# A two-layer diffusion trunk on one Trainium2 core: the last down matrices loaded and used in halves, one token tile's expert rows summed by TensorE, the next norm inside the expert pass, and an opening loaded field by field

## The reference

```python
for i in range(DEPTH):                       # 2 layers
    sh1, sc1, g1, sh2, sc2, g2 = modulation(c, w_ada[i], b_ada[i])
    h = rmsnorm(x, norm_g[i, 0]) * (1 + sc1) + sh1
    y = hgrn2_mixer(h, ...) if i == 0 else diff_attention(...)
    x = x + g1 * y
    h = rmsnorm(x, norm_g[i, 1]) * (1 + sc2) + sh2
    x = x + g2 * hier_moe(h, ...)            # 16 experts, two for each token

def hier_moe(u, ...):                        # w_gate, w_up: (16, 1024, 512); w_down: (16, 512, 1024)
    h = silu(einsum('nd,edf->nef', xt, w_gate)) * einsum('nd,edf->nef', xt, w_up)
    h = h * combine[:, :, None]
    return einsum('nef,efd->nd', h, w_down)
```

## Time and profile before

| | us |
|---|---|
| median of 3 runs (lowest, highest) | 1240.55 (1237.82, 1240.55) |
| the profiled execution | 1240.84 |
| its span | 1239.0 |
| TensorE busy in the span | 1141.3 (92%) |
| VectorE busy | 428.6 (35%) |
| ScalarE busy | 225.6 (18%) |
| GpSimd busy | 136.1 (11%) |
| read from HBM | 304.67 MB |

### The profile page before, as it was taken

How to read it: one execution, slowest core, us unless ns; L and a number is a source line. 1 busy time by engine, 2 the same in 40 slices (tenths; PEclk the granted TensorE clock), 3 DMA queues, 4 the chain that set the end, 5 groups by cost and what they waited for, 6 DMA issues and landing times.

```text
span 1239.0 us, 20044 instructions
## 1 busy us (share of the span) xinstructions
PE 1141.3 (92%) x8612; PEld 681.9 (55%) x8612; DVE 428.6 (35%) x1108; ACT 225.6 (18%) x523; POOL 136.1 (11%) x219
## 2 busy tenths in 40 slices
PE   4999999998899999999989899998989899999885
PEld 2566666665444576666654444444545756666552
DVE  2155555555522350100003755307853420000007
ACT  2210101011111321011000311116632221011010
POOL 0343433333100000000002100000000000000012
PEclk9999999999899999999989899998999999999998
DMA  9973444434923348999999913226751279999993
GB/s 337 316 242 110 138 138 137 137 137 176 380 103 125 136 163 335 424 426 426 424 426 409 346 68 115 106 100 237 262 235 64 73 295 426 426 425 426 424 423 143
DMA packets 97601, 317.08 MB, mean 256 GB/s; under 512 B 3792, under 2 KB 38912, under 8 KB 81120
## 3 DMA queue, kind: packets, MB, share of 16 engines
q1 hardware_dynamic: 90160, 298.05, 62.8%
q10 hardware_dynamic: 5248, 10.97, 2.3%
q0 software_dynamic: 2096, 6.67, 1.5%
HBM read 304.67 MB, written 11.01 MB: 255 GB/s over the span
## 4 chain that ended last, share of the span: by engine, by line
issue 70%; PE 20%; DVE 3%; DMA 3%; POOL 1%; ACT 0%; POOLq 0%; DVEq 0%
PE bank L775 10%; PE bank L784 4%; DMA ring<-expert_rows,moe_row 2%; PE bank L800 2%; PE bank L470 1%; DVE ring L1666 1%; DMA ring<-in_w_ada 1%; PE bank L856 1%; PE bank L809 0%; DVE hg_kf L1759 0%; PE bank L849 0%; DVE uT L1664 0%; PE bank L867 0%; PE bank L476 0%; DVE uT L1676 0%
## 5 line engine op out<-in xcount | busy, mean ns | idle before, releaser
L665 PE MATMUL bank<-ring,xn 128*64 128x256 f32 x1536 | 175.4, 387 | 10.7 <-DMA ring<-in_moe_w_up 7.9
L665 PEld LDWEIGHTS bank<-ring,xn 128*64 128x64 f32 x1536 | 112.1, 140 | 76.5 <-issue 12.8
L775 PE MATMUL bank<-uT,ring 128*128 128x384 f32 x384 | 135.0, 496 | 0.9 <-DVE uT L1712 0.9
L971 PE MATMUL bank<-ring,uT 128*128 128x512 f32 x288 | 126.6, 595 | 1.3 <-issue 1.3
L1654 DVE TENSOR_TENSOR moe_hh<-xn,bank 128x256 f32<-128x256 f32 x32 | 13.5, 421 | 308.0 <-ACT xn L1151 307.9
L2019 POOL TENSOR_TENSOR moe_flag<-con 128x1 f32<-128x1 f32 x2 | 0.4, 192 | 850.8 <-DMA expert_rows<-xn 850.8
L654 PE MATMUL bank<-moe_g,moe_h 128*128 128x128 f32 x768 | 92.2, 277 | 0.4 <-DVE moe_g L1552 0.4
L775 PEld LDWEIGHTS bank<-uT,ring 128*128 128x128 f32 x384 | 69.2, 190 | 42.1 <-issue 2.0
L654 PEld LDWEIGHTS bank<-moe_g,moe_h 128*128 128x128 f32 x768 | 88.2, 192 | 6.1 <-issue 6.1
L971 PEld LDWEIGHTS bank<-ring,uT 128*128 128x128 f32 x288 | 53.9, 191 | 65.4 <-issue 65.4
L681 PE MATMUL bank<-ring,xn 128*64 128x512 f32 x384 | 85.0, 595 | 0.6 <-DMA ring<-in_moe_w_down 0.6
(11 more groups left out here) (269 smaller groups left out, 1306.2 us busy)
## 6 DMA issues: line engine op xcount, KB each, us to landing
ring<-in_w_ada SPq DMA_DIRECT2D x24, 2048.0 KB, 9.9
...
```

The source lines that it names most:

```text
L665: last = mm(bank[2 + e][64 * g:64 * g + 64, 256 * part:256 * part + 256], m["xe"][:, k, 64 * e:64 * e + 64], cols(slot)[:, k, 256 * g:256 ...
L775: last = mm(to[:, 0:TOK], w[:, k, f, :], uT[:, k, :], start=(k == 0), stop=(k == KC - 1))
L971: last = mm(bank[b % 2][:, :], uT[:, k, t * P:(t + 1) * P], cols(slot)[:, k, :], start=(k == 0), stop=(k == KC - 1))
```

## The change

- The eighth pair's two down matrices are loaded in four transfers instead of two: first the columns 0 to 511 of both, then the columns 512 to 1023 (`last_down`). A contiguous piece is 2 KB, where it was 8 KB. TensorE waits for the first two transfers (`down_half`), does the first half, then the last pair's products of the first half (`first_halves`), and waits for the other two before the second half. `keep_busy` ahead of it is 2 products instead of 6.
- The fetched rows of tile 1 are weighted and summed by TensorE: four products (`fetched_rows`) with diagonal matrices `rw` that VectorE builds beside the gate products. GpSimd adds nothing to x any more. VectorE does tile 0 first, then sums tile 2's rows, then finishes tiles 1 and 2 by halves.
- For the first layer the norm of the next layer stands in the pass: ScalarE squares each tile as it is done and takes the root, VectorE normalises, with the columns of the modulation made earlier. TensorE turns tile 0 behind the pass and tiles 1 and 2 within the first two products of the attention's input matrix; eight `keep_busy` products between are gone. ScalarE does both halves of tile 0's shift and scale.
- The first block of the attention's input matrix is issued when the gathers of tile 2 have landed, where it waited only for its buffer.
- The mean goes everywhere: the root takes the sum with a scale and a bias (`root_of`). In three places a root of a constant (`root_table`) stands ahead of the real one.
- Opening: head 0 is loaded as fields q and first gate, then modulation blocks 1 and 3, then the other two fields. TensorE takes block 1 before the head's products, and part 1's later blocks wait for pieces of `uT`.

The core of the diff:

```diff
+            def first_head(fields, landed):
+
+                src = a["hgrn_w_in"][0].rearrange("(k p) (f h n) -> p k f h n", p=P, f=5, h=HEADS)
+                for f in fields:
+                    sp.dma_start(head_cols(4)[:, :, f, :], src[:, :, f, 0, :]).then_inc(landed, 16)
...
+            def last_down(n, p):
+
+                for half in range(2):
+                    here = slice(512 * half, 512 * half + 512)
+                    for e in range(2):
+                        slot, use = expert_slot(n, PAIRS - 1, 4 + e)
+                        if half == 0:
+                            sp.wait_ge(*expert_free(n, PAIRS - 1, 4 + e, p))
+                        src = a["moe_w_down"][n, 2 * (PAIRS - 1) + e].rearrange("(k p) n -> p k n", p=P)
+                        sp.dma_start(down_rows(slot).rearrange("p g j n -> p (g j) n")[:, :, here], src[:, :, here])\
+                            .then_inc(S[n]["down_half"] if half == 0 else full[n][slot], 16)
+
             x_rows = x[:, :, :]
             sp.dma_start(x_rows[:, 0, :], a["x_prompt"][0]).then_inc(x_in, 16)
             sp.dma_start(x_rows[:, 1:3, :], a["x_sample"][0].rearrange("(t p) d -> p t d", p=P)).then_inc(x_in, 16)
             ada(0, 0, 0, 0)
             ada(0, 2, 2, 0)
-            head(0, 4, 0)
+            first_head((0, 2), first_in)
             ada(0, 1, 1, 0)
             ada(0, 3, 3, 0)
+            first_head((3, 1), full[0][4])
             sp.dma_start(masks[:, :, :].rearrange("p n t -> p (n t)"), a["const_mask"]).then_inc(heads_in, 16)
             sp.dma_start(HG["s0"][:, :, :], a["state_hgrn"][0, 0].rearrange("n h p v -> p (n h) v")).then_inc(heads_in, 16)
             head(1, 5, 0)
...
+                if b == 0:
+                    sp.wait_ge(S[0]["rows2"], count * 32)
+                elif slot == SLOT_ORDER[0][0]:
+                    sp.wait_ge(norm_act, count * (2 * T))
+                else:
+                    sp.wait_ge(used[0][slot], count * USES + uses_before[0][slot])
                 src = a["attn_w_qkv"][0].rearrange("(k p) (b n) -> p k b n", p=P, n=512)
                 sp.dma_start(cols(slot), src[:, :, b, :]).then_inc(full[1][slot], 16)
...
                     if i == PAIRS - 1:
-                        keep_busy(6, 512)
-                    rows_of = [down_rows(weights_in(i, 4 + e)) for e in range(2)]
+                        keep_busy(2, 512)
+                        pe.wait_ge(s["down_half"], at_pass[0] * 32 + 32)
+                        rows_of = [down_rows(expert_slot(n, i, 4 + e)[0]) for e in range(2)]
+                    else:
+                        rows_of = [down_rows(weights_in(i, 4 + e)) for e in range(2)]
                     for half in range(2):
+                        if half == 1 and i == PAIRS - 1:
+                            first_halves(it)
+                            for e in range(2):
+                                weights_in(i, 4 + e)
                         for g in range(2):
                             for j in range(2):
                                 for e in range(2):
...
+
+                def last_pair(t, half, start, stop):
+
+                    return mm(bank[LAST_BANKS[t][half]][:, :], m["wc"][:, t * P:(t + 1) * P], m["oe"][:, half, :],
+                              start=start, stop=stop)
+
+                def first_halves(it):
+
+                    pe.wait_ge(s["wc_ready"], at_pass[0] + 1)
+                    pe.wait_ge(s["oe_ready"], it * 2 + 1)
+                    last_pair(0, 0, True, True).then_inc(s["last_mm"], 1)
+                    last_pair(1, 0, True, False)
+                    last_pair(2, 0, True, True)
+
+                def fetched_rows(half):
+
+                    here = slice(512 * half, 512 * half + 512)
+                    for j, rows in enumerate((m["own"], second_rows[n])):
+                        done = mm(bank[LAST_BANKS[1][half]][:, :], m["rw"][:, j, :], rows[:, 1, here],
+                                  start=False, stop=(j == 1))
+                    return done
...
-                    pe.wait_ge(s["wc_ready"], p + 1)
                     pe.wait_ge(s["oe_ready"], p * (2 * PAIRS) + 2 * PAIRS)
-                    for t in range(T):
-                        for half in range(2):
-                            mine = mm(bank[LAST_BANKS[t][half]][:, :], m["wc"][:, t * P:(t + 1) * P], m["oe"][:, half, :],
-                                      start=True, stop=True)
-                        mine.then_inc(s["last_mm"], 1)
-
-                expert_passes(pe, n, before, body, after)
+                    last_pair(0, 1, True, True).then_inc(s["last_mm"], 1)
+                    last_pair(2, 1, True, True).then_inc(s["last_mm"], 1)
+                    last_pair(1, 1, True, False)
+                    pe.wait_ge(s["rows1"], p * 32 + 32)
+                    fetched_rows(0)
+                    fetched_rows(1).then_inc(s["last_mm"], 1)
+
+                return expert_passes(pe, n, before, body, after)
...
+            first_block(2, raw)
             proj(0, 0, 0, 0)
-            proj(0, 0, 0, 2)
-            first_block(2, raw)
             first_turn(2, raw)
             first_block(3, raw)
+            proj(0, 0, 0, 2)
             first_turn(3, raw)
             proj(0, 0, 0, 4)
-            need(pe, 0, "uT_act", T)
-            need(pe, 0, "uT_dve", T)
             for part in (1, 3, 5, 6, 7, 8):
                 proj(0, 0, 0, part)
...
             raw = AT["raw"]
-            keep_busy(8, 512)
-            for t, banks in enumerate(((6, 4), (2, 3), (5, 7))):
-                need(pe, 1, "xn_ready", t + 1)
-                turn_tile(1, "xT_done", xn, t, banks)
+            def turn_features(t):
+
+                pe.wait_ge(norm_dve, count * T + t)
+                turn_tile(1, "xT_done", xn, t, LAST_BANKS[t])
+
+            turn_features(0)
...
+            def root_of(to, sums, count):
+
+                return A(to, sums, ACT.Sqrt, bias=const("eps"), scale=1.0 / count)
+
...
+                def after(p):
+                    if n == 0:
+                        root_table()
+                        for t in range(T):
+                            act.wait_ge(s["added"], p * T + (T + t))
+                            A(second_rows[n][:, t, :], x[:, t, :], ACT.Square, accum_out=stat[:, 0, t:t + 1])\
+                                .then_inc(norm_act, 1)
+                            act.wait_ge(norm_act, p * (2 * T) + (2 * t + 1))
+                            root_of(stat[:, 2, t:t + 1], stat[:, 0, t:t + 1], D).then_inc(norm_act, 1)
+
+                return expert_passes(act, n, before, body, after)
...
+                        for j in range(2):
+                            v.tensor_scalar(m["rw"][:, j, :], ident, m["hw"][:, j, 1:2], None, ALU.mult)
...
+                    def gated_rows(t):
+
+                        other = second_rows[n][:, t, :]
+                        await_step(step(v.tensor_tensor(other, other, gates[:, SIDE[t], :], ALU.mult)))
+                        await_step(step(v.tensor_tensor(x[:, t, :], x[:, t, :], other, ALU.add)))
+
+                    def last_added(t, half):
+
+                        here = slice(512 * half, 512 * half + 512)
+                        other, last_pair = second_rows[n][:, t, here], bank[LAST_BANKS[t][half]][:, :]
+                        dve.wait_ge(s["last_mm"], p * LAST_MM + (2 + half, 5, 4)[t])
+                        if t == 2:
+                            await_step(step(v.tensor_tensor(other, other, last_pair, ALU.add)))
+                            last_pair = other
+                        await_step(step(v.tensor_tensor(other, last_pair, gates[:, SIDE[t], here], ALU.mult)))
+                        added = v.tensor_tensor(x[:, t, here], x[:, t, here], other, ALU.add)
+                        if half == 1:
+                            added.then_inc(s["added"], 1)
+
+                    def next_norm(t):
+
+                        dve.wait_ge(norm_act, p * (2 * T) + (2 * t + 2))
+                        own_root = v.reciprocal(stat[:, 0, 8 + t:9 + t], stat[:, 2, t:t + 1])
+                        own_root.then_inc(s["root_done"], 1)
+                        dve.wait_ge(s["root_done"], p * T + (t + 1))
+                        v.tensor_scalar(xn[:, t, :], x[:, t, :], stat[:, 0, 8 + t:9 + t], None, ALU.mult).then_inc(norm_dve, 1)
+
+                    rows_summed(0)
+                    gated_rows(0)
+                    last_added(0, 0)
+                    last_added(0, 1)
+                    rows_summed(2)
+                    if n == 0:
+                        next_norm(0)
+                    for t in range(1, T):
+                        last_added(t, 0)
+                        last_added(t, 1)
+                    if n == 0:
+                        next_norm(1)
+                        next_norm(2)
```

216 lines of the change are left out of this document (106 added, 110 removed).

## The result

The changed kernel takes 1242.5 us (median of 6, 1237.8 to 1244.1), the kernel before 1238.7 in the same comparison: ratio 1.0032, 95% interval 1.0016 to 1.0048, 3.9 us slower. The profiled execution took 1242.12 us with a span of 1240.3, against 1240.84 and 1239.0. So the two profiles lie only 1.3 us apart where the medians lie 3.8: the profile of the kernel before is one of its slower executions. One execution of a later version (4 KB pieces) took 1963 us at a mean granted clock of 0.556 and is left out of its ratio.

A forecast was written before the change was run, and what follows sets the result against it. TensorE, busy 92% of the span, was taken as the bound; opening -2.1, mean -0.4, first stage end +3.3 and kernel end +2.0 gave +2.8 on 1240.84, so 1243.6 us, range 1236.3 to 1247.5.

The forecast's parts named there:

- the likeliest case: Whole kernel: the forecast of 1243.6 us, with 1241.5 to 1246 for itself and a chance of 0.50.
- Opening: Start of the kernel: the new order removes TensorE's waits, gain 2.1 us, bounds 0 and 2.6.
- the mean: Each layer's second norm: the small mean instruction goes from a chain TensorE waits for, 0.2 us each, 0.4 in sum.
- Rival three: Opening gives nothing because block 3 or the last fields land late: 2.1 us more, 1245.7; chance 0.08.
- When the second halves land: Both stage ends: queues alternate piece for piece, so second halves land at 678 in the first stage, 1219 in the last.
- Rival one: Both stage ends: two 2 KB pieces pass per gather piece, halves land in time, sum -3.7 us, 1237.1; chance 0.27.
- End of the first stage: First expert stage's end to the attention's first product: 3.3 us later, bounds a gain of 3.1 and a loss of 7.7.
- rival two: TensorE's waits at the stage ends let the clock fall for longer: +7.4 us, 1248.2; chance 0.13.
- the branch: End of the first stage: ScalarE's branch that skips further passes, behind the root, taken as 1.4 us.
- End of the kernel: Last stage's end: 1.7 us later plus 0.3 for another possible clock fall, 2.0, bounds -1.9 and +3.5.
- Sum: Whole kernel: -2.1 - 0.4 + 3.3 + 2.0 = +2.8 us on the profiled 1240.84, giving 1243.6.
- the first part: What bounds the kernel now: TensorE busy 92% of the span, its idle time in three places that the change touches.

The follow-up runs named there:

- 4 KB pieces: Changed kernel with the last down matrices split by contraction rows, each piece one 4 KB row instead of 8 KB: 1240.6 us, ratio 1.0026 to the kernel before.
- half of the gathers: Changed kernel with the second of each token's two rows not fetched: 1234.9 us, ratio 0.9980 to the kernel before.

## Why the prediction held, and where it didn't

The forecast was 1243.6, the result 1242.5, inside the likeliest case. That the two lie so close is in part luck. The forecast adds 2.8 to one execution of 1240.84, which it took for 0.3 above the median; against the median of six it stands 2.1 above. The loss on medians is 3.8, so a loss forecast too small was added to a base too high. By its steps:

- **Opening**, 2.1 us (bounds 0 and 2.6), and 0.4 for the mean: the changed kernel was 3.0 ahead at 50 us and 2.4 at the end of the first stage. 0.2 of it stood there before the change could act (28.23 against 28.42, where the second group of transposes starts), so the opening gave 2.8, a little more than its upper bound. The 0.4 can't be seen by itself: the clock was low for 13.7 us from 422 on, in the second norm, where the profile of before has 3.4. Alone the opening gave 1.6 on medians. Rival three is out.
- **When the second halves land**: 678 was forecast; they came at 675.17, which is 677.6 with the 2.4 us of lead added. In the last stage 1219 was forecast, and TensorE started at 1218.69. The turn of one piece for one piece held with 2, 4 and 8 KB, and the landing moved as it says with half of the gathers. Rival one, by which two 2 KB pieces pass in a turn, is refuted, and with it the rule of the Trainium skill as the prediction read it (DMA: Bandwidth & Descriptors, SWDGE vs HWDGE vs iDMA).
- **End of the first stage**, +3.3: 3.0 against the profile that the forecast started from, 5.0 against an execution whose clock was full in the transposes (both above). The wait was 3.24 and 0.7 less than forecast. The falls of the clock took 1.5 (5.14 against 3.65) and 1.8 (8.08 against 6.25), forecast 1.3 and 1.6, so rival two's cost did not come. ScalarE's idle time that the forecast put down to the branch was 1.0 and not 1.4.
- **End of the kernel**, +2.0: measured 1.5 to 1.7.
- **Sum**, +2.8: the profiles differ by 1.3, since 0.8 came back in the attention and the second layer, and since the end of the kernel and the passage each cost a little less; the medians differ by 3.8. Single executions of one kernel lie 6 us and more apart, and the base was a slow one, so the two don't contradict each other.

One reading failed, in the first part: "a copy, six products until 684.3, then VectorE until 694.6". It makes VectorE's last operations wait for TensorE. In the kernel before they wait for VectorE itself, which works from the first fetched rows (672.09 in the first stage, 1212.65 in the last) without a gap above 0.77 us. VectorE in its first stage:

```profile
672.09 0.75 DVE L1664 TENSOR_SCALAR uT<-uT,moe_hw 128x1024 f32<-128x1024 f32 x1 [8.35 <-DMA ring<-expert_rows,moe_row]
...
676.19 2.21 DVE L1664 TENSOR_SCALAR uT<-uT,moe_hw 128x1024 f32<-128x1024 f32 x1 [0.77 <-DMA ring<-expert_rows,moe_row]
...
684.96 1.23 DVE L1669 TENSOR_TENSOR ring<-ring,gates 128x1024 f32<-128x1024 f32 x1
686.11 1.28 DVE L1676 TENSOR_TENSOR uT<-bank,gates 128x512 f32<-128x512 f32 x2
```

The first gating of the last pair's part (L1676) starts as the work on the fetched rows (L1669) ends, 1.8 us behind TensorE's last product at 684.3. The forecast built the chain of the changed kernel anew and compared ends, so the wrong reading entered no term. But it hid what the change is about. It makes TensorE the bound at both stage ends, and in the same edit gives the weights that TensorE waits for 37% of the DMA engines' time instead of 73% (the windows at 2 and 8 KB above), in favour of rows for which VectorE no longer has to hurry. The halves cost nothing where VectorE is the bound (1.0005). With TensorE as the bound, the version whose products all wait for whole matrices is 5.4 us slower than before although the opening gains (1.0044), most of it by the low clock behind its waits, and large pieces with half of the products ahead of the last landing make it 4 faster (0.9968). What the rows by TensorE, the norm within the pass and the fewer `keep_busy` products gain or lose each by itself was not tried.
